# Last up-projection as seven block products on 20 of 22 tile pairs, with down-projection chunks between them

## The reference

```
h = rmsnorm(x, norm_ffn)                                        # 512 x 1024
u = causal_depthwise_conv(h @ w_ffn_up, conv_ffn_w, conv_ffn_b) # 512 x 5632, 3 taps
gate, val = split(u, 2)                                         # 2816 each
x = x + (silu(gate) * val) @ w_ffn_down                         # 2816 -> 1024
return rmsnorm(x, norm_final)
```

## Time and profile before

| | us |
|---|---|
| median of 3 runs | 2801.03 (2799.91 to 2805.11) |
| the profiled execution's own time | 2798.72 |
| its span | 2796.9 |
| PE busy | 2698.8 (96%) |
| DVE busy | 1643.9 (59%) |
| ACT busy | 1213.7 (43%) |
| POOL's DMA queue (q0) | 134.22 MB, 20.3% of 16 engines |
| SP's weight queue (q1) | 249.60 MB, 27.1% |

### The profile page before, as it was taken

The page is one execution under the profiler, slowest core; times in us unless marked ns, Lnnn a source line. Parts: engine busy times, 40 slices in busy tenths (PEclk is TensorE's granted clock), DMA queues, the critical chain, the costliest instruction groups (busy, mean ns, idle before and its releaser), DMA issues.

```text
span 2796.9 us, 41961 instructions
## 1 busy us (share of the span) xinstructions
PE 2698.8 (96%) x16063; PEld 2259.0 (81%) x16063; DVE 1643.9 (59%) x2826; ACT 1213.7 (43%) x1953; POOL 168.6 (6%) x229
## 2 busy tenths in 40 slices
PE   7999999999999999999999999988999999999998
PEld 6877889999889798778898786756877777778786
DVE  3444487265555365486274627765589876665656
ACT  3456455153445344355153524354464454332322
POOL 1110100000000000000000001231000000000000
PEclk9999999999999999999999999999999999999999
DMA  9984736958565563377553134412433333222321
GB/s 350 204 197 106 196 91 217 224 166 248 118 201 178 128 174 120 101 215 218 134 173 119 48 122 133 137 31 80 138 98 113 113 106 106 83 98 90 98 90 68
DMA packets 143564, 393.62 MB, mean 141 GB/s; under 512 B 13080, under 2 KB 13080, under 8 KB 142752
## 3 DMA queue, kind: packets, MB, share of 16 engines
q1 hardware_dynamic: 94256, 249.60, 27.1%
q0 software_dynamic: 46688, 134.22, 20.3%
q10 hardware_dynamic: 2448, 7.41, 0.7%
HBM read 381.62 MB, written 117.56 MB: 178 GB/s over the span
## 4 chain that ended last, share of the span: by engine, by line
PE 82%; DVE 9%; ACT 5%; issue 3%; DMA 1%; ACTq 0%; DVEq 0%; POOL 0%; SPq 0%; POOLq 0%
PE ps L362 41%; PE ps L1454 17%; PE ps L511 5%; PE ps L2233 2%; PE ps L1890 2%; PE ps L869 2%; PE ps L2035 2%; PE ps L1917 2%; PE ps L748 2%; PE ps L2759 1%; DVE w_lo L333 1%; DVE xs L2904 1%; PE ps L835 1%; PE ps L1866 1%; ACT w_hi L325 1%
## 5 line engine op out<-in xcount | busy, mean ns | idle before, releaser
L333 DVE TENSOR_TENSOR w_lo<-raw,w_hi 128x1024 fp32r<-128x1024 f32 x472 | 576.9, 1223 | 442.3 <-ACT w_hi L325 439.2
L325 ACT ACTIVATE w_hi<-raw 128x1024 fp32r<-128x1024 f32 x472 | 497.0, 1055 | 526.3 <-PE ps L362 377.0
L362 PE MATMUL ps<-x_hi,w_hi 128*128 128x512 f32 (+1 forms) x1024 | 383.4, 386 | 32.9 <-DVE w_lo L333 17.3
L362 PE MATMUL ps<-x_lo,w_hi 128*128 128x512 f32 (+1 forms) x1024 | 379.8, 383 | 0.0
L362 PE MATMUL ps<-x_hi,w_lo 128*128 128x512 f32 (+1 forms) x1024 | 377.8, 381 | 0.0
L362 PEld LDWEIGHTS ps<-x_hi,w_hi 128*128 128x128 f32 x1024 | 189.9, 190 | 84.3 <-DVE w_lo L333 25.5
L1454 PE MATMUL ps<-x_hi,w_hi 128*128 128x264 f32 (+1 forms) x800 | 229.1, 286 | 6.6 <-DVE h_z L1555 5.8
L1454 PE MATMUL ps<-x_hi,w_lo 128*128 128x264 f32 (+1 forms) x800 | 228.0, 285 | 0.0
L1454 PE MATMUL ps<-x_lo,w_hi 128*128 128x264 f32 (+1 forms) x800 | 227.6, 285 | 0.0
L362 PEld LDWEIGHTS ps<-x_hi,w_lo 128*128 128x128 f32 x1024 | 189.9, 190 | 38.0
L362 PEld LDWEIGHTS ps<-x_lo,w_hi 128*128 128x128 f32 x1024 | 189.4, 190 | 37.9 <-issue 1.0
(11 more groups left out here) (469 smaller groups left out, 5542.6 us busy)
## 6 DMA issues: line engine op xcount, KB each, us to landing
raw<-in_weights SPq DMA_DIRECT2D x297, 512.0 KB
raw<-weight_sums SPq DMA_DIRECT2D x200, 256.0 KB
weight_sums<-in_weights POOLq DMA_DIRECT2D x30, 1536.0 KB, 19.4
raw<-in_weights SPq DMA_DIRECT2D x150, 256.0 KB
weight_sums<-in_weights POOLq DMA_DIRECT2D x12, 2048.0 KB, 33.9
weight_sums<-weight_sums POOLq DMA_DIRECT2D x10, 1536.0 KB, 14.7
weight_sums<-weight_sums POOLq DMA_DIRECT2D x4, 2048.0 KB, 22.2
steps_abc<-acum_rows POOLq DMA_DIRECT2D x16, 512.0 KB, 5.7
```

What stands on the lines that cost most here:

```text
L325: nc.scalar.activation(w_hi[:, s], raw[:, s], ACT.Copy).then_inc(hi_ready, 1)
L333: nc.vector.tensor_tensor(w_lo[:, s], raw[:, s], w_hi[:, s], ALU.subtract).then_inc(lo_ready, 1)
L362: last = nc.tensor.matmul(o[:, h, :], w[:, s, k], a[:, k0 + k, cols], start=start and k == 0 and n == 0, stop=stop and k == nk - 1 and n == 2)
```

## The change

1. The last part is `gv0` (2 pairs, as before), then `sevenf`: 20 pairs by seven block products (70 chunks) with 16 chunks of the down-projection between them at the block numbers of `MIXED`, then `fd2` (8 chunks). The down-projection's groups are 8, 6 and 8 hidden tiles. DVE adds a down-projection chunk to the residual as it comes (`added`).
2. The first conv tap (with the bias) goes from DVE to ACT (`tap`); DVE keeps two `scalar_tensor_tensor` per tile. Every step of silu, product, `f_hi` and `f_lo` is placed by block number (`self.steps`).
3. 20 more pairs need weight sums, in three groups of 6, 7 and 7 pairs. Their 21 steps stand in `ssm_loads`, two behind each of the first six `steps_abc` loads and one behind each of the next nine.
4. Older sums move: group 5 (`seven1a`) has its last two steps together at `ro1`, and group 6 (`seven1b`) its first two at `ret_out1` in place of `up1a`.

```diff
-STAGES += [s for g, n in enumerate((8, 8, 6)) for s in ((f"gv{g}", 2 * n), (f"fd{g}", 8))]
+STAGES += [("gv0", 4), ("sevenf", 86), ("fd2", 8)]
+MIXED = {"sevenf": (54, 58, 64, 68, 74, 78, 84, 90, 98, 104, 110, 116, 122, 130, 140, 142)}
...
+SUM_GROUPS += [(("seven1a", 0, 6),), (("seven1b", 0, 8),)] + [(("sevenf", a, b),) for a, b in ((0, 6), (6, 13), (13, 20))]
...
+        def copy_one(pool, part, which):
+            row, half = ((1, 0), (0, 0), (1, 0), (0, 1))[which]
+            pool.dma_start(sums_at(part, which), quarters(part, row, half)).then_inc(sums_copied, 16)
...
+        SUM_STEPS = [(FFN_SUMS + n, step) for n in range(3) for step in range(7)]
+        def sums_step(pool, n):
+            group, step = SUM_STEPS[n]
+            if step < 4:
+                copy_one(pool, SUM_GROUPS[group][0], step)
+            else:
+                SUM_PARTS[step - 3](pool, group)
...
-                SUM_PARTS[h](pool, 5)
-            for name, parts in (("up1a", SUM_PARTS[:2]), ("down1a", SUM_PARTS[2:])):
+                for part in ((sums_copy,), (sums_of_two,), (sums_of_three, sums_of_four), ())[h]:
+                    part(pool, 5)
+            for name, parts in (("ret_out1", SUM_PARTS[:2]), ("down1a", SUM_PARTS[2:])):
...
                 pool.dma_start(steps_abc[:, n % 2], src).then_inc(abc_in[n % 2], 16)
+                for step in ((2 * n, 2 * n + 1) if n < 6 else (n + 6,)):
+                    if step < len(SUM_STEPS):
+                        sums_step(pool, step)
...
+            def tap(self, act, f, half):
+                wait(act, hidden_lo, HIDDEN + f - 1 if f > 1 else 0)
+                nc.scalar.activation(self.f_conv[:, slot], self.f_in[:, slot, 2:2 + SEQ], ACT.Identity,
+                                     scale=par[:, w(2)], bias=par[:, b]).then_inc(f_begun, 1)
...
+                first_two(pe, "gv0", x_hi, x_lo, (False, False), rms_ffn.ready, outs=[early_out(t, False) for t in range(2)])
+                for t in (2, 3):
+                    chunk_products(pe, "gv0", Step(t), x_hi, x_lo, False, lead=1)
+                def enter(pe, b, kind, i):
+                    for c in mixed_at("sevenf", b):
+                        self.mixed_pe(pe, c)
+                self.seven_pe(pe, "sevenf", enter)
```

More of the change, by code:

```diff
@@ L58 @@
     if _n in SEVEN:
-        _s += 2 * SEVEN[_n]
+        _s += 2 * SEVEN[_n] + len(MIXED.get(_n, ()))
+        _t += len(MIXED.get(_n, ()))
         _p += SEVEN[_n]
@@ L78, in seven_order, with seven_chunk, mixed_chunk, mixed_at @@
     return order
-SUM_GROUPS = [("seven0a", "seven0b")] + [(f"sevenr{h}",) for h in range(4)] + [("seven1a",), ("seven1b",)]
+def seven_chunk(name, b):
+    return FIRST_CHUNK[name] + b // 2 + sum(p <= b for p in MIXED.get(name, ()))
+def mixed_chunk(name, c):
+    return FIRST_CHUNK[name] + min(MIXED[name][c], 7 * SEVEN[name]) // 2 + c
+def mixed_at(name, b):
+    return [c for c, p in enumerate(MIXED.get(name, ())) if p == b]
+SUM_GROUPS = [(("seven0a", 0, 6), ("seven0b", 0, 8))] + [((f"sevenr{h}", 0, 6 if h else 4),) for h in range(4)]
+SUM_GROUPS += [(("seven1a", 0, 6),), (("seven1b", 0, 8),)] + [(("sevenf", a, b),) for a, b in ((0, 6), (6, 13), (13, 20))]
 def seven_counts(name, reads):
@@ L261, in stream_seven, with inserted @@
         def stream_seven(sp, name):
-            group = [name in names for names in SUM_GROUPS].index(True)
-            sp.wait_ge(sums_added, sums_before(group + 1))
+            last = max(n for n, parts in enumerate(SUM_GROUPS) if name in [part[0] for part in parts])
+            sp.wait_ge(sums_added, sums_before(last + 1))
+            def inserted(b):
+                for c in mixed_at(name, b):
+                    g = mixed_chunk(name, c)
+                    sp.wait_ge(lo_ready, g + 1 - RING)
+                    src = weights[FIRST_SOURCE[name] + 2 * SEVEN[name] + c]
+                    sp.dma_start(raw[:, g % RING, :, :].rearrange("p k n -> p (k n)"), src).then_inc(landed[g % RING], 32)
             for b, (kind, i) in enumerate(seven_order(SEVEN[name])):
-                g, half = FIRST_CHUNK[name] + b // 2, b % 2
+                inserted(b)
+                g, half = seven_chunk(name, b), b % 2
                 s = g % RING
@@ L1115, in program, with __init__ @@
         class Norm:
-            def __init__(self, name, tile, g, last=False, summed=False):
+            def __init__(self, name, tile, g, last=False, summed=False, xc_start=None):
                 self.summed = summed
```

372 lines of the change are left out of this document (276 added, 96 removed).

## The result

| | before | after |
|---|---|---|
| median of the runs | 2800.47 us (4 runs, 2796.83 to 2805.11) | 2820.69 us (4 runs, 2819.43 to 2823.57) |
| ratio, 95% interval | 1 | 1.0073 (1.0055 to 1.009) |
| span of the profiled execution | 2796.9 us | 2821.8 us |
| PE busy, instructions | 2698.8 us, 16063 | 2683.9 us, 16783 |
| SSM: `dec_end` of scan chunk 0 to that of chunk 15 | 2020.14 to 2289.62, 269.5 us | 2013.20 to 2320.56, 307.4 us |

A forecast was written before the change was run, and what follows sets the result against it. PE was taken to bound the kernel (82% of the chain of waits). Terms -24.0 - 3.8 + 6.5 - 5.5 + 42 = +15.2 us on 2798.7 gave 2813.9, median 2816; 8-in-10 range 2780 to 2832 us.

The forecast's parts named there:

- term 1: Last part: 960 matmuls of 512 columns go, 1680 of 256 columns come; -24.0 us.
- term 2: Last part: PE's waits for `f_lo` at the three changes from up to down go; -3.8 us.
- Term 3: Entry into `sevenf` (+4) and its pace up to the first down chunk (+2.5), DVE without reserve; +6.5 us.
- term 4: `seven1a`: moving two accumulating DMAs to `ret_out1` ends late weights and PE's gaps; -5.5 us, bounds 0 and -5.8.
- Term 5: SSM: loads of `steps_abc` behind weight sums on POOL come late for chunks 3, 4 and 6; +42 us.
- loads hidden: SSM: buffers cover late loads, or POOL's DMAs share engines without queueing; late loads cost +12 us or less; chance 0.25.

The follow-up runs named there:

- the run with all three edits: Changed kernel with the weight sums spread outside the SSM, the tail reordered and a split moved behind the seventh sum: 2772.03 us, ratio 0.9899.
- the runs with 4 KB: Changed kernel with `steps_abc` loads as one 4 KB piece per partition: on POOL's queue ratio 1.0045; on ScalarE's queue 2806.09 us, ratio 1.0017.

## Why the prediction was right, and where it was not

The forecast of +15 us for the profiled execution became +24.9 (2796.9 to 2821.8). The direction, the deciding stage and its mechanism were right. The terms:

| term | forecast | measured | from |
|---|---|---|---|
| 1, products | -24.0 | about -22 | last part 351.9 us in the run with all three edits, less its 5.6 us of waits: 346.3, where 372.5 - 24.0 - 3.8 = 344.7 |
| 2, `f_lo` | -3.8 | -3.8, but +7.1 at the same place | no wait for `f_lo`; a new one for `x`, 5.2 us and 1.9 of clock |
| 3, entry and pace | +6.5 | +12.9 | waits of 7.8, 1.4 and 0.7 us, and 3.0 at the lower clock level |
| 4, sums of `seven1b` | -5.5 | -8.4 | two gaps gone, 0.4 left (-5.1), and 3.3 of clock |
| 5, late loads | +42 | +37.9 | SSM 269.5 to 307.4 us |

**Term 5**, which decided, was right in place and mechanism; its size is in part luck, as two errors met. The landings foreseen for loads 3, 4 and 6 (17, 24 and 30 us) came as 17.8, 21.8 and 27.7. The adds for 6 pairs took 25.5 us (2035.18 to 2060.67) where 25.8 were read from the earlier trace rows, those for 7 pairs 27.5 for 30.1. The late times themselves were smaller, 12.55, 5.71 and 12.70 us for 13, 11 and 19. Counted from the start of the SSM, load 4 landed 2.7 us sooner than foreseen and was needed 2.6 us later; load 6 landed 8 us sooner, as its adds started 3.7 us sooner and took 27.5 us. Against these 31 us stand the 38 of the stage: 33 us of idle time and 5 of matmuls at the lower clock level, which the sum had left out. GpSimd's own waits were in the walk (load 3 due at 2056.4 and issued at 2069), and they hold the load back about as much as the queue does (8.9 and 9.8 us for load 3 in the runs with 4 KB). The rival *loads hidden* fell on the three waits; its second half, that POOL's DMAs share the engines and do not queue, on load 3 in the runs with 4 KB: 16.9 us from issue to landing behind the sum in POOL's queue, 7.1 us in ScalarE's, with the same packets.

**The last part** was forecast about 351 us and took 366.5, 15 us more. Nearly half of this, and all that no bound had covered, is one step. **The step that failed** is the one in term 2: "The tail on ACT and DVE behind the last product ... is about 8 us", hidden behind 13 us. I followed the last hidden tile, which `fd2` reads at its eighth block. But the first tile of `fd2` needs the PSUM bank of down chunk 14, and this chunk's residual add stands on VectorE behind the last four convolution rows. PE's timeline, and VectorE's at the same time:
```profile
2753.90 0.40 PE L3248 MATMUL ps<-f_hi,w_lo 128*128 128x512 f32 x1
2759.51 0.79 PE L3248 MATMUL ps<-f_hi,w_hi 128*128 128x512 f32 x1 [5.21 <-DVE x L3384]
2760.10 0.63 PE L3248 MATMUL ps<-f_lo,w_hi 128*128 128x512 f32 x1
```
```profile
2754.13 1.22 DVE L376 TENSOR_TENSOR w_lo<-raw,w_hi 128x1024 fp32r<-128x1024 f32 x1 [3.06 <-ACT w_hi L368]
2755.27 0.68 DVE L3235 TENSOR_TENSOR f_lo<-f_conv,f_hi 128x512 fp32r<-128x512 f32 x1
2755.87 2.98 DVE L2959 SCALAR_TENSOR_TENSOR f_conv<-f_in,par,f_conv 128x512 f32<-128x512 f32 x4
2758.77 0.68 DVE L3384 TENSOR_TENSOR x<-x,ps 128x512 f32<-128x512 f32 x1
```
Chunk 14 was done near 2750, its add ran 9 us later. To the 5.2 us come nine matmuls that start 0.43 us apart (granted clock 0.50 in 2760.5 to 2763 us), where 0.233 is the pace: 1.9 us. The reordered tail gave back 7.3 us in this place. So the instructions cost what the rows say; what went wrong was the walk, which left out the add and its place in the order.

**Term 3** was mis-sized, inside its bounds. The waits of the entry came as walked (1.41, 0.7 and 1.74 us for +4). The pace was taken as an even 0.3 us a pair; it came as single waits every other pair (1.25, 1.83, 1.84 us), in which a split stood ahead of the sum that PE needed, and another of 1.12 us at the end. One of them, on DVE and on PE:
```profile
2522.90 1.22 DVE L376 TENSOR_TENSOR w_lo<-raw,w_hi 128x1024 fp32r<-128x1024 f32 x1
2524.04 0.42 DVE L3398 SCALAR_TENSOR_TENSOR f_in<-ps,f_fifth 128x256 f32<-128x256 f32 x1
```
```profile
2524.51 0.39 PE L1505 MATMUL ps<-x_hi,w_hi 128*128 128x256 f32 x1 [1.83 <-DVE f_in L3398]
```
Averages of busy time (9.9 against 9.9 us a pair) could not show this; the order of two instructions did, and turning them round gave 6.7 us, part of it by the clock.

**The clock** is missing from every term. I priced a wait at its length. Behind the waits the granted clock was at the lower level for some time, in the SSM (0.50 in 2086 to 2090 us of after), in `seven1a` of before, at the entry and in the pace of `sevenf`, and at `fd2`. That is 5.0, 3.3, 3.0 and 1.9 us, and because of it term 4 lies outside its own bound of -5.8, which counted the waits alone.

Together, terms 2 and 3 cost 13.5 us that the forecast did not have, term 1 saves 1.6 us less, and terms 4 and 5 come 7.0 us under theirs: +23.3 us by this table. The other 1.6 us are lost in the profiled execution between 1880 and 1900 us, where executions of the same code differ by as much. The median of the runs moved by 20.2 us where 15.2 were forecast, and part of that closeness is owed to terms 4 and 5 making up for 2 and 3.
